# Attention probabilities left unscaled on their way to TensorE, the softmax factors multiplied onto the product with V, in a two-block fp32 kernel

## The reference, cut to what matters

```python
m = jnp.max(s, axis=-1, keepdims=True)
e = jnp.exp(s - m)
l = jnp.sum(e, axis=-1, keepdims=True)
o = jnp.einsum('brnqhk,brnkhd->brnqhd', e / l, vb.astype(jnp.float32))
lse = (m + jnp.log(l))[..., 0]
...
wts = jax.nn.softmax(jnp.stack(lses, axis=0), axis=0)
o = jnp.concatenate([outs[g] * wts[g][..., None] for g in range(len(DIL_PATTERNS))], axis=2)
...
h = h + jnp.concatenate([pool_out, attn_out], axis=-1) @ w_out[i]
```

## Time and profile before

| | before |
|---|---|
| median of 3 runs (lowest, highest) | 1379.98 us (1376.84, 1380.45) |
| the profiled execution: time, span | 1383.31 us, 1381.5 us |
| TensorE matmul busy | 1296.9 us, 94% |
| VectorE busy | 826.3 us, 60% |
| ScalarE busy | 640.7 us, 46% |
| GpSimd busy | 127.8 us, 9% |
| mean granted TensorE clock | 0.973 of full |
| layer 0, start of v0 to start of the output projection | 57.86 to 116.90 us |
| layer 1, the same | 431.98 to 513.07 us |

### The profile page before, as it was taken

How to read it: one execution, slowest core, us unless ns; L and a number is a source line. 1 busy time by engine, 2 the same in 40 slices (tenths; PEclk the granted TensorE clock), 3 DMA queues, 4 the chain that set the end, 5 groups by cost and what they waited for, 6 DMA issues and landing times.

```text
span 1381.5 us, 22278 instructions
## 1 busy us (share of the span) xinstructions
PE 1296.9 (94%) x9198; PEld 1188.4 (86%) x9198; DVE 826.3 (60%) x1189; ACT 640.7 (46%) x950; POOL 127.8 (9%) x110
## 2 busy tenths in 40 slices
PE   6989999999989999789999989988889998999997
PEld 6968888888889789679999979988789998999996
DVE  5785554444786845676655686577645566644444
ACT  6354534443566544433444446454235453544443
POOL 1220000000001301140001030023310000000000
PEclk9999999999999999899999999999999999999999
DMA  9545687776646242334534444543004555455540
GB/s 315 180 128 177 214 273 246 273 256 237 212 162 186 67 153 92 122 122 139 164 126 153 153 129 123 146 123 112 10 1 152 183 168 169 141 188 189 186 151 31
DMA packets 164571, 219.46 MB, mean 159 GB/s; under 512 B 5401, under 2 KB 135287, under 8 KB 164343
## 3 DMA queue, kind: packets, MB, share of 16 engines
q1 hardware_dynamic: 162610, 215.88, 48.2%
q10 hardware_dynamic: 1860, 2.16, 0.5%
HBM read 216.19 MB, written 1.05 MB: 157 GB/s over the span
## 4 chain that ended last, share of the span: by engine, by line
PE 60%; issue 21%; DVE 8%; ACT 3%; DVEq 2%; POOL 2%; POOLq 2%; DMA 2%; ACTq 1%; SPq 0%
PE bank L535 17%; PE bank L537 16%; PE bank L536 16%; DVE w_lo L526 2%; PE bank L598 2%; PE bank L1313 1%; PE bank L820 1%; PE bank L1291 1%; PE bank L1515 1%; DVEq L2165 1%; PE bank L808 1%; ACT w_hi L517 1%; DMA arena<-in_vec_rows 1%; DVE arena L2205 1%; PE bank L1298 1%
## 5 line engine op out<-in xcount | busy, mean ns | idle before, releaser
L526 DVE TENSOR_TENSOR w_lo<-w_raw,w_hi 128x1024 fp32r<-128x1024 f32 (+1 forms) x350 | 424.5, 1254 | 192.8 <-ACT w_hi L517 186.4
L535 PE MATMUL bank<-act_hi,w_hi 128*128 128x256 f32 x1744 | 505.0, 290 | 16.8 <-DVE act_lo L2133 5.1
L536 PE MATMUL bank<-act_lo,w_hi 128*128 128x256 f32 x1744 | 498.5, 286 | 0.0
L537 PE MATMUL bank<-act_hi,w_lo 128*128 128x256 f32 x1744 | 498.2, 286 | 0.0
L517 ACT ACTIVATE w_hi<-w_raw 128x1024 fp32r<-128x1024 f32 (+1 forms) x350 | 348.9, 1041 | 119.1 <-PE bank L537 97.3
L535 PEld LDWEIGHTS bank<-act_hi,w_hi 128*128 128x128 f32 x1744 | 339.6, 195 | 31.0 <-issue 19.9
L536 PEld LDWEIGHTS bank<-act_lo,w_hi 128*128 128x128 f32 x1744 | 339.8, 195 | 1.0 <-issue 0.5
L537 PEld LDWEIGHTS bank<-act_hi,w_lo 128*128 128x128 f32 x1744 | 339.6, 195 | 0.0
L535 PE MATMUL bank<-w_hi,side_hi 128*128 128x512 f32 (+1 forms) x392 | 152.3, 388 | 0.5 <-DVE w_lo L526 0.5
L537 PE MATMUL bank<-w_hi,side_lo 128*128 128x512 f32 (+1 forms) x392 | 149.1, 380 | 0.0
L536 PE MATMUL bank<-w_lo,side_hi 128*128 128x512 f32 (+1 forms) x392 | 148.8, 380 | 0.0
(11 more groups left out here) (322 smaller groups left out, 1529.5 us busy)
## 6 DMA issues: line engine op xcount, KB each, us to landing
w_raw<-in_w_in SPq DMA_DIRECT2D x40, 1024.0 KB, 5.7
w_raw<-in_w_up SPq DMA_DIRECT2D x32, 1024.0 KB, 5.5
w_raw<-in_w_down SPq DMA_DIRECT2D x32, 1024.0 KB, 5.0
w_raw<-in_w_mod SPq DMA_DIRECT2D x24, 1024.0 KB, 5.3
w_raw<-in_w_ffn_in SPq DMA_DIRECT2D x22, 1024.0 KB, 5.1
w_raw<-in_w_gate SPq DMA_DIRECT2D x20, 1024.0 KB, 5.2
w_raw<-in_w_ffn_out SPq DMA_DIRECT2D x11, 1024.0 KB, 4.9
w_raw<-in_w_out SPq DMA_DIRECT2D x8, 1024.0 KB, 7.3
```

The source lines that it names most:

```text
L526: nc.vector.tensor_tensor(wlo[:, slot, 0:n], raw[:, st.slot(name), n * half:n * (half + 1)], whi[:, slot, 0:n].bitcast(F32), ALU.subtract) ...
L535: nc.tensor.matmul(o, ahi, bhi, start=start, stop=False, skip_group_check=True)
L536: nc.tensor.matmul(o, ahi, blo, start=False, stop=False, skip_group_check=True)
L537: return nc.tensor.matmul(o, alo, bhi, start=False, stop=stop, skip_group_check=True)
```

## The change

The probabilities are no longer multiplied by the factors before they are turned, so T needs only the exponentials. New entries F spread the factors of two heads over 64 partitions each (four matmuls of a broadcast factor column with the identity, into a low bank). ScalarE copies the product with V into a buffer `cat_t` (four of them), and a new entry H multiplies that by the spread factors on VectorE, copies the high half on ScalarE and subtracts on VectorE, from SBUF now. On TensorE each lot of scores stands ahead of a V projection, u and v2 move into the list `ATT`, T takes the banks of v0 and v1 in turn, and mod and ctx take those of u and v2. The maxima of a pair of heads are scaled together, so exponentials wait for pairs. The places of the splits move. Two semaphores are merged into others.

```diff
+    def many(kind, *n):
+        return [(kind, pairs[i]) for i in n]
+    out = T(0) + [("u", 0)] + T(1) + [("v2", 0)] + many("V", 0, 1) + T(2) + T(3) + many("F", 0, 1) + extra.get(0, [])
+    out += many("H", 0) + many("V", 2, 3) + many("H", 1) + T(4) + T(5) + many("F", 2) + extra.get(1, [])
+    out += many("H", 2) + many("V", 4, 5) + extra.get(2, []) + [("pool", 0)] + many("F", 3, 4, 5) + extra.get(3, [])
+    out += many("H", 3) + extra.get(4, []) + many("H", 4)
+    return out + extra.get(5, []) + many("H", 5) + extra.get("V", [])
...
 ATT_EXTRA = (
-    {1: mod(0, 1), 2: [("modr", 0)] + mod(2, 3), 3: [("modc", 0)], 4: [("modr", 1)], 5: [("modc", 1)]},
-    {1: [("ctx", 0)], 2: [("ctx", 1)], 3: [("conv", 0), ("ctx", 2)], 4: [("conv", 1), ("ctx", 3)], 5: [("conv", 2)],
+    {0: mod(0, 1), 1: [("modr", 0)] + mod(2, 3), 2: [("modc", 0)], 3: [("modr", 1)], "V": [("modc", 1)]},
+    {0: [("ctx", 0)], 1: [("ctx", 1)], 2: [("conv", 0)], 3: [("ctx", 2)], 4: [("conv", 1), ("ctx", 3)], 5: [("conv", 2)],
      "V": [("conv", 3), ("ba", 0)]})
...
-                b = C("v0")
-                project_tokens(pe, (layer, 6), b)
                 scores(0)
-                b = C("v1")
-                project_tokens(pe, (layer, 7), b)
+                v_bank = [C("v0")]
+                project_tokens(pe, (layer, 6), v_bank[0])
                 scores(1)
-                b = C("u")
-                project(pe, (layer, 8), lambda m: (b, T * m), KT, in_hi, in_lo)
+                v_bank.append(C("v1"))
+                project_tokens(pe, (layer, 7), v_bank[1])
                 scores(2)
+                turned, beside = ring(v_bank), None
...
+                    elif kind == "F":
+                        wait("fac_ready", H_ORDER.index(x) // 3 + 1, 2)
+                        b = CL(f"fac{x}")
+                        for t in range(TT):
+                            for i in range(2):
+                                mm = nc.tensor.matmul(ps[b][HEAD * i:HEAD * (i + 1), P * t:P * (t + 1)],
+                                                      fac_of(x, i, t).broadcast_to([P, HEAD]), ident,
+                                                      start=True, stop=True, skip_group_check=True)
+                        full(mm, b)
...
-                        if layer != CTX_LAYER and i == 9:
+                        if layer != CTX_LAYER and i == 11:
                             split_hi(act, chunk(layer, 10), (0,))
-                        if layer == CTX_LAYER and i == 5:
+                        if layer == CTX_LAYER and i == 7:
+                            split_hi(act, chunk(layer, 10))
+                        if layer == CTX_LAYER and i == 11:
                             split_hi(act, chunk(layer, 11))
                     elif kind == "V":
+                        n = H_ORDER.index(x)
+                        if n >= 4:
+                            wait("cat_act", n - 3, 7)
                         b = W(f"pv{x}")
-                        nc.scalar.activation(xhi[:, 2 + x, :], ps[b][:, 0:T], ACT.Copy).then_inc(S("cat_hi"), 1)
+                        free(nc.scalar.activation(cat_t[n % 4], ps[b][:, 0:T], ACT.Copy), b)
+                        act.drain().then_inc(S("cat_o"), 1)
+                    elif kind == "H":
+                        n = H_ORDER.index(x)
+                        wait("cat_t", n + 1, 6)
+                        nc.scalar.activation(xhi[:, 2 + x, :], cat_t[n % 4], ACT.Copy).then_inc(S("cat_hi"), 1)
...
-                    dve.drain()
-                    for hd in heads(batch):
-                        g, i = hd // HPG, hd % 2
-                        for t in range(TT):
-                            e = prob[:, hd, P * t:P * t + P * (t + 1)]
-                            ins = v.tensor_scalar(e, e, fac[:, g, batch, i, t:t + 1], None, ALU.mult)
-                        ins.then_inc(S("prob_ready"), 1)
+                    dve.drain().then_inc(S("fac_ready"), 1)
+
+                def weighted(x):
+
+                    n = H_ORDER.index(x)
+                    b = W(f"fac{x}")
+                    wait("cat_o", n + 1, 6)
+                    free(v.tensor_tensor(cat_t[n % 4], cat_t[n % 4], ps[b][:, 0:T], ALU.mult), b)
+                    dve.drain().then_inc(S("cat_t"), 1)
```

More of the change, by code:

```diff
@@ L245, in attention_order, with T @@
 def attention_order(layer):
-    pairs = [(b, g) for b in range(2) for g in range(3)]
+    pairs = [2 * g + b for b in range(2) for g in range(3)]
     extra = ATT_EXTRA[layer]
[L249 to L259, removed]
+    def T(n):
+        b, g = divmod(n, 3)
+        return [("T", HPG * g + 2 * b), ("T", HPG * g + 2 * b + 1)]
+    def many(kind, *n):
[5 more added lines that the diff above has]
+    return out + extra.get(5, []) + many("H", 5) + extra.get("V", [])
 def mod(*chunks):
@@ L277 @@
 V_ORDER = [x for k, x in ATT[0] if k == "V"]
-CAT_ORDER = [2 + x if k == "V" else 0 for k, x in ATT[0] if k in ("V", "pool")]
+CAT_ORDER = [2 + x if k == "H" else 0 for k, x in ATT[0] if k in ("H", "pool")]
+H_ORDER = [x for k, x in ATT[0] if k == "H"]
 def up_at(j):
@@ L1256, in two_blocks @@
         dn_row = early(16)[0:1, :]
-        mod_rows = [Arena(turned_at)(4, 512)[:, i, :] for i in range(4)]
+        mod_rows = [Arena(turned_at)(4, 512)[:, 2 + i, :] for i in range(2)]
+        cat_t = [Arena(turned_at)(4, T)[:, i, :] for i in range(4)]
         A = Arena()
@@ L1408, in _ @@
                         i = T_ORDER.index(x)
-                        wait("prob_ready", i + 1, 12)
-                        b = C(f"pT{x}") if i < 2 else CL(f"pT{x}")
+                        wait("prob_ready", HEADS.index(x) + 1, 12)
+                        b = banks.claim(pe, (layer, f"pT{x}"), turned())
                         e = prob[:, x, :]
@@ L1624, in mod_copy @@
                 act.wait_ge(direct_done, st.direct["mod", 2 * j + 1] + 1)
-                nc.scalar.activation(mod_rows[j % 4], ps[banks.bank(f"mod{j}")][:, :], ACT.Copy).then_inc(S("mod_copied"), 1)
+                nc.scalar.activation(mod_rows[j % 2], ps[banks.bank(f"mod{j}")][:, :], ACT.Copy).then_inc(S("mod_copied"), 1)
             def rms(b, n, scale, out, power=-0.5, bias=eps_col):
@@ L2247, in _ @@
                         dve.drain().then_inc(S("conv"), 1)
-                    if kind not in ("V", "pool"):
+                    if kind not in ("H", "pool"):
                         continue
+                    if kind == "H":
+                        weighted(x)
                     if n == 3 and layer == CTX_LAYER:
                         split_lo(dve, chunk(layer, 11))
-                    if n == 5 and layer != CTX_LAYER:
+                    if n == 3 and layer != CTX_LAYER:
                         split_lo(dve, chunk(layer, 10), (0,))
```

67 lines of the change are left out of this document (38 added, 29 removed).

## The result

| | before | after |
|---|---|---|
| median (lowest, highest) | 1381.12 us (1375.41, 1383.66), 10 runs | 1387.76 us (1384.47, 1392.15), 10 runs |
| the profiled execution: time, span | 1383.31, 1381.5 us | 1387.98, 1386.0 us |
| layer 0: start of its output projection, and of that one's second half | 116.90, 119.8 us | 107.89, 113.85 us |
| layer 1: end of the q and k projections | 431.98 us | 426.28 us |
| layer 1: context product 0 | 470.88 us | 468.55 us |

The kernel became slower: ratio 1.0045, 95% interval 1.0028 to 1.0063, which is 6.6 us between the medians. The forecast was 1388.0 (range 1379.5 to 1395), which is +8.0 on a base of 1379.98 from 3 runs; over 10 runs that base is 1381.12.

A forecast was written before the change was run, and what follows sets the result against it. TensorE, busy 94% of the span, was taken as the bound. Layer 0 at -5.5 and layer 1 at +13.5 gave +8.0: the profiled 1383.3 becomes 1391.3, the median 3.3 below it 1388.0 us (range 1379.5 to 1395).

The forecast's parts named there:

- Layer 0, -5.5: Layer 0: the twelve-instruction multiplication leaves the way; the output projection's second half is ready at 114.3, not 119.8, gaining 5.5 us.
- the 5.03 us hole: TensorE's idle in layer 0 of before, while VectorE multiplies probabilities; predicted to go, with about 1.5 us of slow clock.
- Layer 1, start, +2.7 at context product 0: Layer 1's first scores wait for banks ScalarE empties, delaying v0; context product 0 starts at 473.6 against 470.88.
- Layer 1, chunk 11: ScalarE's wait for chunk 11 delays copies and convolution 0: 8.4 us TensorE idle, 1.6 low clock; layer 1 loses 13.5.
- both shifts one to one: After both stretches TensorE is at its work, so -5.5 and +13.5 pass fully into the total, +8.0 us.
- The port rule: VectorE's subtraction, now with two SBUF inputs, is exposed to GpSimd: at most one doubled, 0.5 us, hidden.
- Rival 1: Layer 1: the stall at chunk 11 doesn't hold TensorE; layer 1 loses 4 to 5, total 1379; chance 0.19 with Rival 5.
- Rival 3: Layer 0: ScalarE becomes the bound through twelve more operations; gain down to 1 or 2, sum +12, 1392; chance 0.11.
- Rival 2: Both layers: layer 0's hole goes in full, 8 us, layer 1's waits mostly hidden; sum -7, 1373; chance 0.08.
- Rival 4: Layer 0: VectorE's last H chain meets GpSimd and doubles, 1.5 us more lost, 1389.5; chance 0.02.
- Rival 5: Both layers: the shifts cancel, layer 0 at -7, layer 1 at +8, no change; chance 0.19 with Rival 1.

The follow-up runs named there:

- experiment 1: Kernel after, with ScalarE's and VectorE's splits of chunk 11 in layer 1 moved behind context convolution 1: 1379.88 us, ratio 0.9980 to before.
- experiment 2: Kernel after, with TensorE's old order in layer 1 (v0 ahead of the first scores): 1386.50 us, ratio 1.0033 to before.
- experiment 3: Kernel after, with both splits of chunk 11 later and v0 first in layer 1: 1376.14 us, ratio 0.9961 to before.
- experiment 5: Kernel after, with every F matmul issued twice: 1388.69 us, ratio 1.0052 to before.
- experiment 6: Kernel after, with only ScalarE's high split of chunk 11 moved, behind convolution 0's middle: 1381.37 us, ratio 1.0008 to before.
- experiment 8: Kernel before, with both splits of chunk 11 in layer 1 moved behind convolution 1: 1380.58 us, ratio 0.9989 to before.
- experiment 4: Kernel before, without multiplying the probabilities by the factors and nothing in its place (output unscaled): 1370.90 us, ratio 0.9924 to before.
- experiment 7: On top of experiment 3, layer 0's second half of chunk 10 split earlier and VectorE's last three products back to back: 1376.06 us, ratio 0.9957 to before.

## Why the prediction was right

It was right in size and sign, and by its two main steps: the gain in layer 0, and the larger loss in layer 1 by ScalarE's wait at chunk 11. That the 1388.0 hit the 1387.76 so closely is luck. The base was 1.1 us too low and the shift 1.4 too large (+8.0 forecast, +6.6 measured), and inside layer 1 two terms were off in opposite directions.

- **Layer 0, -5.5 (bounds -2 to -8).** Measured at the end of layer 1's q and k projections: 426.28 - 431.98 = -5.7 (-5.9 when both are read at the same point). Other executions of the same layer 0 put a width to that: experiments 1, 2, 3, 5 and 6 come there at 426.2 to 428.5, and experiment 8, which is the kernel before up to here, at 435.47, so the shift lies between 3.5 and 9.3 us. The prediction priced the slow clock behind the 5.03 us hole with 1.5 us from one execution; in experiment 8 the same hole is followed by 0.50 from 105.5 to 115.5 us, and the output projection starts 1.8 us later. The second half of the output projection starts at 113.85; the working said 114.3. Its start at 109.2 was 1.3 too late (9.0 us earlier than before, where 6 to 8 was the sign named), since six F cost 0.51 each and not 0.7, a term of 1.1 us. That mis-sizing cost nothing, because the hole behind it (2.78, foreseen as 2 us) took it up, which experiment 5 shows from the other side.
- **Layer 1, start, +2.7 at context product 0.** Measured 42.3 - 38.9 = +3.4. Score pairs, the copies of the turned context as their releaser and the low clock of v0 are as written; v0 itself starts 6.9 us in, where the list had 6.0.
- **Layer 1, chunk 11.** With t the end of product 1, the list had product 2 at t + 13.2 and the output projection at t + 33.8. Measured with t = 487.5: 11.35 and 32.4. The load took 5.23 us where the row of before had 6.83, which is 1.6 of the 1.85. The idle was 6.2 us, not 8.4, the low clock behind it 3.0 us, not 1.6. The two errors are of opposite sign, which is luck, and the shift at the output projection came out at 93.6 - 81.1 = +12.5, forecast +13.5.
- **The sum.** -5.7 + 13.0 (101.9 - 88.9) = +7.3 us at 528.15 us. The span ends only 4.5 us later, the medians differ by 6.6. The later stretches run the same instructions, but where the clock falls in them differs from execution to execution, by a few us in sum (the 29 runs of before beside experiments 1 to 4 lie between 1375.6 and 1385.5). The step "both shifts one to one" holds only to within these.
- **The port rule.** One subtraction with two SBUF inputs met GpSimd, which works until 96.31 us, and took 0.72 us where the others take 0.42 to 0.43; the product with one PSUM input right behind it kept 0.42. The prediction looked at the new operations only. One of the small products that make the factors met it too (L2224, two SBUF inputs): it took 1.18 us at 88.64, beside GpSimd, and 0.16 at 75.63 without it. That chain ends at 90.8 us and the first F starts at 92.56, so it cost nothing here.

```profile
94.21 0.72 DVE L2294 TENSOR_TENSOR act_lo<-arena,act_hi 128x256 fp32r<-128x256 f32 x1 [0.53 <-ACT act_hi L1819]
95.13 0.42 DVE L2239 TENSOR_TENSOR arena<-arena,bank 128x256 f32<-128x256 f32 x1 [0.19 <-issue]
```

  GpSimd's row beside it:

```profile
93.14 3.17 POOL L2596 TENSOR_TENSOR arena<-arena 64x256 f32<-64x256 f32 x4
```

  The Trainium skill ("SBUF — State Buffer", Who interferes with whom) says that a VectorE instruction with two SBUF inputs contends with a GpSimd instruction that reads SBUF, and one with at most one SBUF input doesn't. These rows agree, and the 0.29 us lay off the path.

Rival 1 (the stall doesn't hold TensorE) fell by the chain, and experiment 1 gives the stall's price: 7.9 us (9.0 by the ratios). Rival 3 (ScalarE the bound of layer 0) fell: T waits 0.42 to 0.67 us for its copies, but u, v2 and the mod products lie between. Rival 2's mechanism, the waits hidden and the hole gone, is what experiment 3 built in part: it gives 0.9961 where the rival gave 1373 of 1380 (0.9949), and a 2.79 us hole is left in either layer. Rival 4 (the port rule at the last H chain) fell, since GpSimd ends 11 us before that chain starts. Rival 5 (no change) fell by the interval, which starts at 1.0028.

What stays open: experiment 2 saves 5.7 us in layer 1's stretch, its span is 3.3 shorter and the median shows 1.3; experiment 4 saves 9.9 us up to the end of layer 1 and its span is 14.0 shorter. How much of either is the clock in the second block wasn't taken apart. Nor was layer 0's part timed in a kernel of its own.

## What to carry to other kernels

When an order is changed, look at each wait on an in-order queue that was harmless, and list again what is now queued behind it: ScalarE's 14 us at a load cost 0.6 us in the medians, 3.3 at most, while two 7 us products covered it, and its 12 us cost 8 when the copy of a PSUM bank that TensorE claims next stood behind it. Price a stall with the clock behind it. Work added in front of a wait is nearly free (0.9 us for six more F in each layer), and a wait removed may only move to the next operand: follow both to the next join before adding their prices up.

## What the runs showed of the hardware

- The granted clock behind 4.86 + 1.30 us of idle stood at 0.50 in two whole stretches of 5 us, although TensorE was busy throughout the second; products 2 and 3 lost 3.0 us. With F doubled in that stall, at the low clock too, and no second hole, TensorE was busy without a break from 497.19, the clock was back at 502.2, and the loss was 0.7. The Trainium skill ("TensorE: Matmul & The Clock Gate", What's actually happening) says that activity releases the throttle; these two runs agree.
- A hole of the same length doesn't cost the same clock. Behind the 2.79 us hole of layer 0 the stretch from 114 to 120 us had PEclk 1.00 in after and experiments 2 and 3, 0.73 in experiment 6 and 0.72 in experiment 1, where layer 1 then starts 2.2 us later than in after, with the same instructions up to there.

```profile
114.00:120.00 6.00, 5.60 (x34) 0.72 0.77 239
```

- The output projection of layer 1 has no idle ahead of it in any of the kernels, behind the small product `ba` (32 matmul records with 16 columns), and still takes 5.8 us in experiments 1, 2 and 4, 7.3 in 3 and 5 to 8, 7.8 in before and 8.3 in after. The difference is how much of it runs at 0.41 us a product and how much at 0.28. What decides it wasn't found.
- The same 1 MB load of chunk 11 took 6.83 us in before, 6.3 in experiment 4 and 6.9 in experiment 8, and 4.9 to 5.3 in after and the other six. In the three slow ones its last 1.2 to 1.8 us move only 20 to 26 GB/s, about a sixteenth of the 350 to 390 in its middle, as if one of the 16 DMA engines finished late. These three, and none of the others, have a fetch on the instruction queue q14 (0.01 MB) in the same 8 us. Whether that fetch is the cause isn't shown.
